# The chunked WKV recurrence of a decoder step: three groups of TensorE matmuls cut to 64x64 corners, two GpSimd products replaced by ScalarE copies, and a new order of the loop

## What is computed

```python
def wkv7_scan(r, w, k, v, a, b, s0):
    def step(S, inp):
        rt, wt, kt, vt, at, bt = inp
        S = (S * wt[:, :, None, :] + jnp.einsum('bhvk,bhk->bhv', S, at)[..., None] * bt[:, :, None, :]
             + vt[..., None] * kt[:, :, None, :])
        return S, jnp.einsum('bhvk,bhk->bhv', S, rt)
```

## Time and profile before

| | us |
|---|---|
| median of 3 runs | 3282.68 |
| the runs | 3276.82, 3282.68, 3298.46 |
| the profiled execution's own time | 3257.57 |
| its span | 3255.9 |
| TensorE busy over the span | 3060.6 (94%) |
| VectorE, ScalarE, GpSimd busy | 1614.8, 915.1, 1403.8 |
| mean granted TensorE clock, of full | 0.969 |
| the recurrence in the span | about 1842 to 2378 |

### The profile page before, as it was taken

The page is one execution under the profiler, slowest core; times in us unless marked ns, Lnnn a source line. Parts: engine busy times, 40 slices in busy tenths (PEclk is TensorE's granted clock), DMA queues, the critical chain, the costliest instruction groups (busy, mean ns, idle before and its releaser), DMA issues.

```text
span 3255.9 us, 71713 instructions
## 1 busy us (share of the span) xinstructions
PE 3060.6 (94%) x31500; PEld 2880.4 (88%) x31500; DVE 1614.8 (50%) x2107; ACT 915.1 (28%) x1528; POOL 1403.8 (43%) x1046
## 2 busy tenths in 40 slices
PE   7999989989999999979999899999988999999997
PEld 6989856989999999969999777878878999999996
...
GB/s 100 119 134 109 151 169 116 81 96 61 79 79 111 79 137 137 56 69 113 142 91 91 91 76 77 63 62 59 36 172 97 59 79 79 111 79 137 137 43 62
DMA packets 342464, 312.14 MB, mean 96 GB/s; under 512 B 35335, under 2 KB 303059, under 8 KB 341020
## 3 DMA queue, kind: packets, MB, share of 16 engines
...
## 4 chain that ended last, share of the span: by engine, by line
PE 43%; DVE 6%; issue 2%; ACT 1%; SPq 1%; DMA 1%; POOL 0%; ACTq 0%; DVEq 0%; POOLq 0%
PE PS L521 17%; PE PS L688 12%; PE PS L2807 2%; PE PS L2819 1%; PE PS L2813 1%; PE PS L2801 1%; PE PS L2887 1%; DVE act_lo L2516 1%; PE PS L2797 1%; PE PS L702 1%; PE PS L2793 1%; PE PS L2922 1%; PE PS L2873 0%; PE PS L2891 0%; SPq L496 0%
## 5 line engine op out<-in xcount | busy, mean ns | idle before, releaser
L521 PE MATMUL PS<-act_hi,w_hi 128*128 128x344 f32 x1992 | 640.8, 322 | 33.8 <-DVE act_lo L2150 16.8
L521 PE MATMUL PS<-act_lo,w_hi 128*128 128x344 f32 x1992 | 637.1, 320 | 0.0
L521 PE MATMUL PS<-act_hi,w_lo 128*128 128x344 f32 x1992 | 636.7, 320 | 0.0
L502 POOL CAST w_hi<-w_raw 128x1024 fp32r<-128x1024 f32 (+1 forms) x119 | 129.2, 1086 | 1074.5 <-PE PS L521 560.5
L521 PEld LDWEIGHTS PS<-act_hi,w_hi 128*128 128x128 f32 x1992 | 375.9, 189 | 39.6 <-issue 24.2
L521 PEld LDWEIGHTS PS<-act_lo,w_hi 128*128 128x128 f32 x1992 | 375.9, 189 | 0.0
L521 PEld LDWEIGHTS PS<-act_hi,w_lo 128*128 128x128 f32 x1992 | 375.9, 189 | 0.0
L688 PE MATMUL PS<-T,wq_S 128*128 128x258 f32 x2880 | 365.7, 283 | 0.0
L688 PE MATMUL PS<-act_hi,wq_A 128*128 128x258 f32 x1920 | 364.5, 282 | 0.0
L688 PEld LDWEIGHTS PS<-T,wq_S 128*128 128x128 f32 x2880 | 354.4, 189 | 0.0
L688 PEld LDWEIGHTS PS<-act_hi,wq_A 128*128 128x128 f32 x1920 | 305.4, 190 | 0.0
...
## 6 DMA issues: line engine op xcount, KB each, us to landing
...
```

What stands on the lines that cost most here:

```text
L502: nc.gpsimd.tensor_copy(w_hi[:, u, 0:kts, :], w_raw[:, u, 0:kts, :]).then_inc(w_hi_done, 1)
L521: mm = nc.tensor.matmul(PS[:, 3 * u + c, 0:CH], w[:, u, kt, :], x[:, kt, CH * c:CH * c + CH], start=(kt == 0 and part == 0), stop=(kt == k ...
```

## The change

**Matmuls.** `g_AK` is strictly triangular, so its corner of rows 64 to 127 against columns 0 to 63 is zero. `g_AK` v now is three matmuls with 64x64 weights for each head instead of one with 128x128, and `f_A` S four for each pair instead of two with 64x128. The rows' half goes to bank 6 or 7, both heads of a pair side by side. `pX64` of the same item is interleaved with the three corners, as it uses the fourth 64x64 tile. One matmul with the zero corner of `m_incl` as weights starts the accumulation of a quarter that would have had no `start`. `pX32` is interleaved over three 32x32 tiles.

```diff
@@ scan_tensor
-                    for q in range(GP):
-                        for e in range(2):
-                            mm(PS[:, 6 + e, DH * q:DH * q + DH], g_AK[:, x, GP * e + q, :], t_V[:, n % 3, P * q + DH * e:P * q + DH * e + DH],
-                               start=(q == 0), stop=False, skip_group_check=True)
-                    for q in range(GP):
-                        for e in range(2):
-                            ins = mm(PS[:, 6 + e, DH * q:DH * q + DH], f_A[half(e), x, q, :], S[half(e), q, :],
-                                     start=False, stop=True, skip_group_check=True)
+                    pe.wait_ge(BA.sem, BA.of("t64", n))
+                    pe.wait_ge(BA.sem, BA.of("x21", n))
+                    pe.wait_ge(BA.sem, BA.of("xd", n))
+                    S = state(n)
+                    mm(PS[half(0), 7, 0:GP * DH], nothing, S[half(1), :, :].rearrange("p q v -> p (q v)"), start=True, stop=False, skip_group_check=True)
+                    for h in range(GH):
+                        V = [t_V[half(a), n % 3, P * (h % GP) + DH * (h // GP):P * (h % GP) + DH * (h // GP) + DH] for a in range(2)]
+                        for a, b in ((0, 0), (1, 1), (0, 1)):
+                            mm(part(h, a, b), g_AK[half(a), n % 2, h, half(b)], V[a], start=(h == 0), stop=False, skip_group_check=True)
+                        ins = mm(PS[half(0), 3, DH * h:DH * h + DH], i_T64[half(1), h, :], i_XT[half(1), h, DH:P], start=True, stop=True)
+                    ins.then_inc(BP.sem, BP.turn("pX64", n))
                     for q in range(GP):
-...
+                        for e, b in ((0, 0), (1, 1), (0, 1), (1, 0)):
+                            ins = mm(part(GP * e + q, e, b), f_A[half(e), n % 2, q, half(b)], S[half(e), q, :], start=False, stop=True, skip_group_check=True)
                     ins.then_inc(BP.sem, BP.turn("pAS", n))
```

```diff
@@ scan_vector
-                    nc.vector.tensor_copy(q_rhs[:, :, :, :].rearrange("p e q v -> p e (q v)"), PS[:, 6:8, 0:DH * GP]).then_inc(BV.sem, BV.turn("rhs", n))
+                    dve.wait_ge(BA.sem, BA.of("rhs7", n))
+                    tt(flat(q_rhs), PS[:, 6, :], flat(q_rhs), ALU.add).then_inc(BV.sem, BV.turn("rhs", n))
```

```diff
@@ scan_gpsimd
-                    tt(i_Xa[:, :, :].rearrange("p h (r t) -> p h r t", t=32), spread(0, 2), on_diagonal(2), ALU.mult).then_inc(BG.sem, BG.turn("xad", i))
-                    tt(i_XT[:, :, :].rearrange("p h (r t) -> p h r t", t=32), spread(1, 4), on_diagonal(4), ALU.mult).then_inc(BG.sem, BG.turn("diag", i))
@@ scan_scalar
+                    for b in range(2):
+                        ins = nc.scalar.copy(i_Xa[quad(b), :, quad(b)], i_X[quad(b), n % 2, 0, :, :])
+                    ins.then_inc(BA.sem, BA.turn("xa", n))
...
+                    for b in range(4):
+                        ins = nc.scalar.copy(i_XT[quad(b), :, quad(b)], i_X[quad(b), n % 2, 1, :, :])
+                    ins.then_inc(BA.sem, BA.turn("xd", n))
```

**Order.** All four strings change; on GpSimd `f_kp` moves from the step of p into that of s, `f_b` comes before the masking of `g_RK`, and `f_R` is last:

```diff
-        BG = Order(sem("sc_pool"), "rk:s rkm:i R:s b:s xad:i diag:i sum:o kp:p o:o", AHEAD, -3, ITEMS + 1, ITEMS)
+        BG = Order(sem("sc_pool"), "kp:s rk:s b:s rkm:i sum:o o:o R:s", AHEAD, -3, ITEMS + 1, ITEMS)
```

More of the change, by code:

```diff
@@ L2903, in scan_tensor @@
+                    pe.wait_ge(BG.sem, BG.of("R", i))
+                    pe.wait_ge(BV.sem, BV.of("ak", i))
+                    scores(0, f_B, f_R[:, i % 3, :, :]).then_inc(BP.sem, BP.turn("pRB", i))
+                    pe.wait_ge(BA.sem, BA.of("t2", i))
+                    if i:
+                        pe.wait_ge(BV.sem, BV.of("tr", i - 1))
+                    level_X(i).then_inc(BP.sem, BP.turn("pX2", i))
                 if live_s:
@@ L3037, in scan_scalar @@
                 if live_n:
-                    act.wait_ge(BP.sem, BP.of("pT64", n))
-                    nc.scalar.copy(wide(i_T64[half(1), :, :]), PS[half(1), 2, :]).then_inc(BA.sem, BA.turn("t64", n))
+                    act.wait_ge(BP.sem, BP.of("pX32", n))
+                    if n:
+                        act.wait_ge(BP.sem, BP.of("pU", n - 1))
                     for b in (0, 2):
@@ L3042, in scan_scalar @@
                     ins.then_inc(BA.sem, BA.turn("x21", n))
+                    act.wait_ge(BP.sem, BP.of("pT64", n))
+                    nc.scalar.copy(wide(i_T64[half(1), :, :]), PS[half(1), 2, :]).then_inc(BA.sem, BA.turn("t64", n))
                 if live_s:
-                    act.wait_ge(in_a[x], 64 * (s // 2 + 1) + START)
+                    act.wait_ge(in_a[s % 2], 64 * (s // 2 + 1) + START)
                     if s:
@@ L3221, in scan_vector @@
                        m_lev[:, :, :].rearrange("p l (o t) -> p l o t", o=1).broadcast_to([P, 5, GH, 32]), ALU.mult).then_inc(BV.sem, BV.turn("ct", i))
-                    dve.wait_ge(BP.sem, BP.of("pAK", i))
-                    tt(g_AK[:, i % 2, :, :], two_banks(0), every(m_strict, GH), ALU.mult).then_inc(BV.sem, BV.turn("ak", i))
-                    dve.wait_ge(BV.sem, BV.of("ct", i))
-                    tt(i_X[:, i % 2, 1, :, :], i_C[:, 0, :, :], every(m_ic, GH), ALU.add).then_inc(BV.sem, BV.turn("xi", i))
-                    dve.wait_ge(BV.sem, BV.of("xi", i))
-                    nc.vector.transpose(wide(i_X[:, i % 2, 0, :, :]), wide(i_X[:, i % 2, 1, :, :])).then_inc(BV.sem, BV.turn("xt", i))
                 if live_o:
+                    new = q_S[:, o % NG, (o // NG + 1) % 2, :, :]
                     dve.wait_ge(BV.sem, BV.of("st", o))
@@ L3234, in scan_vector @@
                     tt(f_cs[:, :, :], f_cs[:, :, :], column(c_mid[:, s % 4, :]).broadcast_to([P, GP, P]), ALU.subtract).then_inc(BV.sem, BV.turn("cc", s))
+                if live_i:
+                    dve.wait_ge(BV.sem, BV.of("ct", i))
+                    tt(i_X[:, i % 2, 1, :, :], i_C[:, 0, :, :], every(m_ic, GH), ALU.add).then_inc(BV.sem, BV.turn("xi", i))
+                piece(1)
                 if k == -1:
```

416 lines of the change are left out of this document (208 added, 208 removed).

## The result

The changed kernel takes 3235.86 us (median of 4 runs, 3225.94 to 3240.03), the kernel before beside it 3285.67 (3276.82 to 3298.46). The ratio is 0.9844, 95% interval 0.9813 to 0.9875: faster by 50 us. The forecast was 3252 with a range from 3234 to 3277; the likeliest case put 30 us on the change, so 20 us came on top of it.

What follows compares the result with a forecast made beforehand. TensorE's own queue was taken as the bound. Terms summed to -1.8 us a full-clock step, 27 over 15 steps, 30 with the last, less 0.5 for memsets; from the median 3282.68 that gave 3252 us, range 3234 to 3277.

Steps and rivals of the forecast that it cites:

- the likeliest case: Whole kernel: 1.8 us saved a full-clock step, 30 us in all, giving 3252 us, own range 3242 to 3263; 54%.
- The block: TensorE's corner matmuls with `pX64` and `f_A` S: 2.3 us instead of 4.04, saving 1.75 a step.
- The rule against it: Corner block: weight loads overlap only across row groups, so two tiles at a time and 0.4 us saved; not followed.
- The two-tile rival: Corner block takes 3.6 us, a step saves 0.5, the kernel takes 3274 us; 12%.
- the one in which tiles don't overlap: Corner block takes 6.9 us at 67 ns a pass, a step loses 2.9, the kernel takes 3329 us; 3%.
- Hidden copies: ScalarE's four `i_XT` diagonal copies before `pT64`: 2.4 us under 2.7 of TensorE work, 0.3 to spare.
- This saves nothing directly: GpSimd losing its two diagonal products: TensorE doesn't wait for GpSimd, so no direct gain, only VectorE time back.
- The wait for `f_K` before `pAK`: TensorE waits 0 to 1.0 us for VectorE, up to 1 more after a long `f_cs`; 0.35 taken as mean.
- moves cost nothing by themselves: New order: moves only change what TensorE does during hand-overs; waits of 0.45 and 0.35 added, 0.47 removed a step.
- The last step: Last full step, at the low clock: block and extra hop save 2.5 us, `pX32` 0.8.
- Everything fits: Rival: passes at 17 ns, opener free, no wait but before `pT16`; 2.85 us saved a step, 3236 us; 12%.
- VectorE's queue: Rival: it bounds nine steps, waits of 1.5 to 2 us before `pT32` and `pAK`, 3266 us; 14%.

Runs made afterwards that it cites:

- e_split2: Changed kernel with `t_K` v moved back between `pX8` and the turns of v, and without the opening matmul: ratio to before 0.9835.
- e_both: Kernel before, in its old order, with the corner block and ScalarE's six diagonal copies in place of GpSimd's two products: ratio 0.9996.
- e_corners: Kernel before, in its old order, with the corner block alone and `rhs7` copied on ScalarE; GpSimd's diagonal products stay: ratio 1.0017.
- e_pooldiag: Changed kernel with only the diagonal products put back on GpSimd, first in its step: ratio to before 0.9965.
- c_after: The changed kernel once more, unchanged, for a second profile: 3224.39 us, ratio to before 0.9836.
- e_rearly: Changed kernel with `f_R` moved from the end of GpSimd's step to behind `f_rk`: ratio to before 0.9852.
- e_order: Changed kernel with whole `g_AK` v and `f_A` S and GpSimd's diagonal products again; new order and three-tile `pX32` stay: ratio to before 1.0145.

## Why the prediction was right, and where it wasn't

- **The block.** Forecast 2.3 us, measured 1.97 in nearly every step. The 64 passes of corners and `pX64` come four in 0.056 to 0.06 us, 14 to 15 ns each, under the lower bound of 17 that I had set from one tile's 67 ns divided by four; those of `f_A` S cost 18 ns (e_split2) to 23. So 67 ns divided by the number of tiles is no lower bound. The opener was 0.5 in the forecast and is 0.41: the block is 1.56 in e_split2, where it is left out.
- **The rule against it.** By the Trainium skill (TensorE: Matmul & The Clock Gate, Part 3: Packing small matmuls, The mechanism) a weight load overlaps only where its row group differs, and I had worked out 3.6 us for that case. The trace doesn't agree: 1.97 us. The two-tile rival and the one in which tiles don't overlap are out.
- **`pX32`.** Forecast 0.6, measured 0.63.
- **GpSimd's products.** Hidden copies: right, no wait of TensorE for ScalarE before `pT64` is in the waits of after. "This saves nothing directly" was right for the old order (e_both against e_corners) and wrong as a statement on the change: in the new order TensorE would wait 2.3 us a step for the products. Not all of that wait is lost, since "issue" is smaller beside it: at full clock the 15 steps are 8 to 15 us longer and the whole kernel some 16. With the low level it is 46 us (e_pooldiag against c_after). The cover that had hidden them is used up by the new order; I had worked out the cover for ScalarE's copies and not for what they replace. VectorE got faster, `c_mid` from 1326 ns on average to 608, `f_cs` from 2817 to 2198, `f_K` from 1380 to 1002, but only `f_K` by the cause that was named: with GpSimd's products back (e_pooldiag) `f_K` takes 1353, `c_mid` 362 and `f_cs` 2066. In the old order the products had been what slowed the first two (e_both: 170 and 1224); in the new one they stand beside GpSimd's `f_R` and `o` instead. With `f_R` moved away (e_rearly) `c_mid` takes 158 and `f_K` 676, and the kernel isn't faster: VectorE isn't what a step waits for. The memsets are 1.5 us instead of 0.5, on GpSimd, where nobody waits.
- **The new order.** The wait for `i_X` before `pT16`: forecast 0.4 to 0.5, in the rows 3.1 / 9 = 0.34. A wait for `q_rs` before the turns of v, 1.5 / 9 = 0.17, wasn't forecast; together they are the 0.5. The wait for `f_K` before `pAK`, forecast 0.35: not seen. Waits for `g_AK` are gone as forecast.
- **Issue.** Forecast 0.05 us a step more for 25 more matmuls. Between before and after it is -0.3 to 0.3 by the profile taken (16.6 and 18.0 to 20.6 and 14.2), so the sum wasn't hurt; but this is luck of the order, not a small price. The same 25 matmuls in the old order cost 1.5 us a step (e_corners), nearly the 1.7 that they save. This step of the argument, "moves cost nothing by themselves", is the one that failed in kind: a move changes how densely the instructions lie, and the supply has a pace.
- **The sum.** A steady full-clock step (steps 3 to 12) is 28.6 to 29.1 instead of 30.7: 1.6 and 2.1 less, forecast 1.8. The size is right, its division isn't: the forecast had nearly all of it from the block and nothing from the copies, while e_order, e_pooldiag and c_after show about half from each.
- **The clock.** The term that was missing. The forecast took the profiled execution of before, with few falls of the clock, and carried the difference in full-clock time to the median. But the changed kernel has less low-clock time, 23 us of the 54 between the means of c_after and of the kernel before beside it. That it has less is an effect of the change, clear of the scatter of the runs (118 with a standard deviation of 10, against 95 with 4); that shorter holes are the reason fits the counts above and is argued, not shown. So it is partly luck that 3235.86 lies in the range, 2 us above its lower end: the forecast had the low level only in the last step, and there as staying. The price of a fall stood in the rows of before only for the last step, and I had asked only there what the change does to it. The last step is the plainest: forecast 3.3 us less, measured 27.1 to 17.5 and 26.8 to 18.9 us, of which 11.9 and 8.5 are the low level that is no longer there; at full clock it is 0.7 to 2.3 us longer.
- **The rivals.** "Everything fits" (3236) met the number, for another reason than it gave: its 2.85 us a step at full clock wasn't reached (1.6 to 2.1). VectorE's queue is no bound (23.6 of 28.7 us).

What stays open: what sets off the fetch of a block of instructions, and so why some borders have a hole of 0.3 us and others of 2.4. The packet behind a long hole isn't slower, it starts later: it takes about 1.1 us with short holes and long. A rival that no run tests is other traffic: in the two profiles of before all 13 issue holes of 1.3 us or more ahead of the last step fall where other transfers move 85 to 278 GB/s (from 2 us before the hole to its end), while the mean of the steady part is 50. Open too is why the last step has no low level after the change.
